# Opening of a two-layer backbone kernel: tokens loaded first, scale row before shift row, first block's products on unshifted tokens

## The chip, the cores and the metric

The kernel runs on 1 core of one Trainium2 chip. The metric is device time in microseconds (us) of that core. Three runs of the kernel before gave 941.29, 941.98 and 942.39, so the median is 941.98. TensorE (PE), VectorE (DVE), ScalarE (ACT), GpSimd (POOL) and SyncE (SP) each run their own instruction stream and wait for each other by semaphores.

## The reference, cut to what matters

Two layers over 256 latent and 256 context tokens of width 1024. The change concerns the start of layer 0 only:

```python
def modulate(h, shift, scale):
    return h * (1.0 + scale) + shift

mod_l = (c_act @ mod_w[i] + mod_b[i]).reshape(b, N_MOD, 1, d)      # latent tokens
mod_c = (c_ctx_act @ mod_w[i] + mod_b[i]).reshape(N_MOD, d)        # context tokens
hl = modulate(rms_norm(xl, norm_g[i, 0]), mod_l[:, 0], mod_l[:, 1])
hc = modulate(rms_norm(xc, norm_g[i, 0]), mod_c[0], mod_c[1])
u = h @ w_in                                                       # 1024 x 1536
y = a * jax.nn.sigmoid(g)            # a: columns 0..511 of u, g: columns 512..1023
# depthwise convolution of y, 31 taps, then layer_norm and silu;
# the last 512 columns of u go through a pooling mixer
# [y_conv | y_pool] @ w_out, gated residual, then a mixture of 32 experts; layer 1 follows
```

So each sub-layer needs a shift row (mod row 0) and a scale row (mod row 1), for latent and for context tokens, and each row is a product of the conditioning vector with a 1024 x 1024 matrix of 4 MB.

## The kernel before, in words

**Weights.** SP issues one stream of loads, in the order of `stream_plan`, nearly all of 2 MB. A unit `("mod", L, v, h)` is half of the matrix of mod row v of layer L; `("win", j)` is a third of the input matrix. The first seven units go into the seven slots of a ring at once; each later one waits until the products that read its slot are done (`slot_plan` picks the slot, the list `early` orders the first ones; `freed` names the semaphore). The four token tiles of 0.5 MB go down the same queue, behind the first unit.

**Opening.** PE turns the small parameter rows into columns (L1018 to L1020). ACT makes the sigmoid of the conditioning vectors (L1510), DVE turns it into their silu `cs` (L1882). ACT squares the tokens (L1522), POOL makes the reciprocal norms (L2266, L2267), DVE scales the tokens by them (L1931), PE turns them (`turn_pair`, L1096), and ACT and DVE copy the turned halves to `hT` (L1635, L2193). Between these PE makes the mod rows (`mod_part`, L1046, 8 products a unit), ACT copies a row (`mod_copy`, L1528), PE turns it (`mod_turn`, L1056), DVE adds the bias (`mod_columns`, L1890) and makes the scale `gsc` (L1924). Then ACT (even k, L1641) and DVE (odd k, L2201) apply scale and shift to `hT` in place, in eight instructions each.

**First block.** `value_gate(m, part)` makes 8 products of 128 x 128 x 512 for value (part 0) or gate (part 1) of channel block m (L1384; the profile counts two MATMUL records for each such product). ACT makes the sigmoid (L1649), DVE multiplies (L2208), and then runs the 31 taps of the convolution on DVE (L2217, L2219 and 29 times L2221) and adds the two accumulators (L2224). There are four blocks m, one after the other. PE meanwhile makes the products of the other blocks, the mod rows 2 to 5 and the pool part (L1397). POOL does the pooling (L2359 to L2365) while DVE is in its taps. When the last block is done, PE turns the result (L1448), DVE and POOL normalise, ACT applies silu (L1687, L1688), and PE makes the output product (L1437); routing and the experts follow.

Each engine works strictly in the order in which its part of the program is written out.

## Time and profile before

| what | value |
|---|---|
| median of 3 runs | 941.98 us (941.29 to 942.39) |
| profiled execution, its own time | 943.45 us |
| its span | 941.8 us |
| PE busy | 838.4 us (89%) |
| DVE busy | 364.3 us (39%) |
| ACT busy | 168.2 us (18%) |
| POOL busy | 178.0 us (19%) |
| chain of waits that ended last | PE 47%, DMA 24%, DVE 13% |
| read from memory | 293.67 MB, 325 GB/s over the span |

A row of a timeline gives start, length, engine, line, operation, what it writes and reads, how many, and in brackets the idle time of the engine before it with what ended it. "PEclk" is the granted TensorE clock as a share of 2.4 GHz, so 1.00 is 2.4 GHz and 0.50 is 1.2 GHz.

### The profile page before, as it was taken

To read this page: it belongs to the slowest core of one execution; us is meant where nothing else is said; L and a number is where in the kernel's file an instruction comes from. 1 tells how busy PE (TensorE), PEld (TensorE's weight loads), DVE (VectorE), ACT (ScalarE), POOL (GpSimd) and SP (SyncE) were. 2 spreads that over 40 slices of the span, in tenths; PEclk is the share of its full clock that TensorE was granted. 3 is DMA by queue.
4 is the path that set the end of the run, shared out by engine and by line. 5 is a ranking of instruction groups with operands and counts; after the bars stand their busy time and mean duration, and the time that the engine had idled before them with its cause. 6 is when DMAs were issued, how large, how long until landed. Compare 5 with 4: busy or idle time off the path is not lost.

```text
span 941.8 us, 10008 instructions
## 1 busy us (share of the span) xinstructions
PE 838.4 (89%) x3727; PEld 371.6 (39%) x3727; DVE 364.3 (39%) x764; ACT 168.2 (18%) x415; POOL 178.0 (19%) x214
## 2 busy tenths in 40 slices
PE   4899999999999999878849999889899999778785
PEld 2444445447433333222228444446445333222221
DVE  1269998217111221110223686648625111011010
ACT  2301012216100000000023111538323000000000
POOL 2100292131120222201131221400211111011001
PEclk9899999999999999999959999989999999889899
DMA  8999355617999999999989459310577999999994
GB/s 364 408 400 407 127 212 216 276 81 261 333 405 410 356 403 399 393 397 416 423 312 429 190 209 366 148 81 1 203 305 249 405 404 406 413 418 427 408 418 174
DMA packets 34038, 297.99 MB, mean 316 GB/s; under 512 B 6624, under 2 KB 6930, under 8 KB 16316
## 3 DMA queue, kind: packets, MB, share of 16 engines
q1 hardware_dynamic: 26928, 283.26, 74.7%
q0 software_dynamic: 6976, 13.93, 4.2%
q8 instruction: 38, 0.62, 0.3%
q14 instruction: 20, 0.16, 0.0%
q10 hardware_dynamic: 76, 0.02, 0.0%
HBM read 293.67 MB, written 12.58 MB: 325 GB/s over the span
## 4 chain that ended last, share of the span: by engine, by line
PE 47%; DMA 24%; DVE 13%; issue 5%; SPq 4%; ACT 3%; PEld 2%; POOL 1%; PEldq 0%; DVEq 0%; POOLq 0%; ACTq 0%
PE bank L1287 12%; DVE WORK L2221 10%; PE bank L496 9%; DMA ring<-in_gu_pack 8%; DMA ring<-in_down_pack 6%; PE bank L1312 5%; PE bank L1437 5%; DMA WORK<-in_gu_pack 4%; DMA ring<-in_win_pack 3%; PE bank L1162 3%; SPq L987 2%; PE bank L1384 2%; DMA h_rows<-B 1%; PE bank L553 1%; PE bank L562 1%
## 5 line engine op out<-in xcount | busy, mean ns | idle before, releaser
L1287 PE MATMUL bank<-ring,hT 128*64 128x512 f32 x704 | 217.4, 629 | 25.6 <-DMA ring<-in_gu_pack 12.9
L2135 DVE SCALAR_TENSOR_TENSOR hT<-hT,WORK,bank 128x256 f32<-128x256 f32 x34 | 16.3, 481 | 323.5 <-ACT hT L1587 310.8
L1287 PEld LDWEIGHTS bank<-ring,hT 128*64 128x64 f32 x704 | 63.9, 144 | 123.6 <-issue 122.9
L2221 DVE SCALAR_TENSOR_TENSOR WORK<-WORK,par 128x512 f32<-128x512 f32 x116 | 90.7, 861 | 0.0
L496 PE MATMUL bank<-ring,hT 128*128 128x512 f32 (+2 forms) x256 | 88.0, 499 | 0.7 <-ACT hT L1550 0.7
L1312 PE MATMUL bank<-ring,WORK 128*64 128x512 f32 x336 | 76.4, 596 | 4.3 <-DMA ring<-in_down_pack 3.3
L1287 PE MATMUL bank<-WORK,hT 128*64 128x512 f32 x128 | 63.7, 644 | 5.0 <-issue 3.5
L1592 ACT ACTIVATE WORK<-bank 128x256 f32<-128x256 f32 x34 | 13.0, 383 | 282.7 <-PE bank L1296 282.7
L1384 PE MATMUL bank<-hT,ring 128*128 128x512 f32 x128 | 58.9, 620 | 1.9 <-DMA ring<-in_win_pack 1.9
L496 PEld LDWEIGHTS bank<-ring,hT 128*128 128x128 f32 x256 | 46.0, 190 | 35.8 <-issue 34.0
L1437 PE MATMUL bank<-ring,B 128*128 128x512 f32 x128 | 56.6, 596 | 0.8 <-DVE B L2238 0.8
L869 POOL DMA_INDIRECT hT<-h_rows,smalli x21 | 20.1, 958 | 174.3 <-PE bank L1261 81.0
L1287 PE MATMUL bank<-X,hT 128*64 128x512 f32 x104 | 46.9, 595 | 5.2 <-DMA B<-in_gu_pack 2.8
L2266 POOL TENSOR_SCALAR small<-small 128x1 f32<-128x1 f32 (+2 forms) x46 | 13.5, 293 | 181.2 <-DVE small L1751 62.1
L1287 PE MATMUL bank<-B,hT 128*64 128x512 f32 x96 | 43.6, 597 | 1.0 <-issue 1.0
L1046 PE MATMUL bank<-ring,cs 128*32 128x512 f32 x256 | 33.9, 666 | 9.1 <-DMA ring<-in_mod_pack 7.8
L1312 PEld LDWEIGHTS bank<-ring,WORK 128*64 128x64 f32 x336 | 23.1, 137 | 47.0 <-issue 40.3
L1384 PEld LDWEIGHTS bank<-hT,ring 128*128 128x128 f32 x128 | 25.1, 199 | 34.2 <-issue 31.2
L882 POOL DMA_INDIRECT latents<-WORK,smalli x8 | 8.2, 1024 | 153.2 <-DVE WORK L2153 153.2
L2267 POOL TENSOR_TENSOR small<-small,cst 128x1 f32<-128x1 f32 (+2 forms) x46 | 35.7, 777 | 3.8
L1437 PEld LDWEIGHTS bank<-ring,B 128*128 128x128 f32 x128 | 23.8, 190 | 31.2 <-issue 27.7
L1587 ACT ACTIVATE hT<-bank 128x256 f32<-128x256 f32 x34 | 13.0, 383 | 125.0 <-PE bank L1287 121.1
(312 smaller groups left out, 1083.3 us busy)
## 6 DMA issues: line engine op xcount, KB each, us to landing
ring<-in_gu_pack SPq DMA_DIRECT2D x39, 2048.0 KB, 19.6
ring<-in_mod_pack SPq DMA_DIRECT2D x24, 2048.0 KB, 14.1
ring<-in_down_pack SPq DMA_DIRECT2D x19, 2048.0 KB, 31.9
WORK<-in_gu_pack SPq DMA_DIRECT2D x6, 2048.0 KB, 23.6
ring<-in_wout_pack SPq DMA_DIRECT2D x4, 2048.0 KB, 12.7
ring<-in_gu_pack SPq DMA_DIRECT2D x8, 1024.0 KB, 28.5
ring<-in_win_pack SPq DMA_DIRECT2D x3, 2048.0 KB, 37.2
X<-in_gu_pack SPq DMA_DIRECT2D x3, 2048.0 KB
```

What stands on the lines that cost most here:

```text
L496: mm = pe.matmul(dst[:, 0:hi - lo], hT[:, k, t * P:(t + 1) * P], w[:, k, :], start=k == 0, stop=k == KC - 1)
L869: return pool.indirect_dma_start(XG[s], None, h2d[:, :], bass.IndirectOffsetOnAxis(ap=smalli[0:ST, i:i + 1], axis=0), bounds_check=rows_ - ...
L987: sp.dma_start(dst, src).then_inc(sem(f"weights_in{at}"), 16)
L1046: mm = pe.matmul(bank[b][at:at + 32, :], cs[:, k, :], w, start=k < 2, stop=k >= KC - 2)
L1162: mm = pe.matmul(bank[OUT_BANKS[L][i % 2]][:, :], lhs(k, j), w[:, k, :], start=k == 0, stop=k == KC - 1)
L1287: mm = pe.matmul(dst[ST * x:ST * x + ST, :], HG[L][s][:, k, :], columns(units[x], 512 * k, 512), start=k == 0, stop=k == KC - 1)
L1312: mm = pe.matmul(bank[5 + s][ST * h:ST * h + ST, :], HET[s][:, f, ST * x:ST * x + ST], columns(n, 2048 * x + 1024 * f + 512 * h, 512), sta ...
L1384: mm = pe.matmul(b[:, :], w[:, k, 256 * part + P * (m % 2):256 * part + P * (m % 2) + P], hT[:, k, :], start=k == 0, stop=k == KC - 1)
L1437: mm = pe.matmul(bank[OUT_BANKS[0][i % 3]][:, :], mixT[:, (k + 4) % KC, j * P:(j + 1) * P], w[:, (k + 4) % KC, :], start=k == 0, stop=k == ...
L2135: dve.scalar_tensor_tensor(out=T1[L][s], in0=SG[L][s], scalar=cwt[:, at:at + 1], in1=src[:, 0:DE], op0=ALU.mult, op1=ALU.mult).then_inc(se ...
L2221: ins = dve.scalar_tensor_tensor(out=acc, in0=src, scalar=w, in1=acc, op0=ALU.mult, op1=ALU.add)
L2267: pool.tensor_tensor(dst, dst, C("half", 0, 1).to_broadcast([P, n]), ALU.pow).then_inc(sem(name), 1)
```

## The change

The stream of loads now begins with the tokens, then mod row 1 (scale), the first input unit, mod row 0 (shift), and the other two input units. `hT` gets only the scale at first. Block 0's products run on these unshifted tokens; the shift's own product with the weights of block 0 is made apart (`shift_products`: 8 products of 32 x 256; `shift_columns`: two of 128 x 2) and added per column in the sigmoid's bias and in the multiplication. The shift is then added to `hT` by ACT and DVE for the later blocks. Mod row 0 is multiplied in the middle of `value_gate(0, 0)`. On ACT the sigmoid of the conditioning now stands behind the four squares.

```diff
-    out = pair(0, 0) + pair(0, 1)
-    out += [("win", j) for j in range(3)]
+    out = pair(0, 1) + [("win", 0)] + pair(0, 0) + [("win", 1), ("win", 2)]
...
             for n, u in enumerate(STREAM):
-                if n == 1:
+                if n == 0:
                     for i in range(NT):
...
-            mod_multiply(0)
             turn_pair("a0", 0, range(KC))
+            pe.wait_ge(sem("par_ready"), 2)
+            mod_half(0, 0)
+            turn_pair("a0", 1, range(KC))
+            busy(5, 12)
+            mod_half(0, 1).then_inc(sem("mod_mm"), 1)
             mod_turn(0)
-            turn_pair("a0", 1, range(KC))
-            mod(1)
...
+            def shift_products():
+                pe.wait_ge(sem("mod_cols"), 2)
+                w = slot(where[("win", 0)])
+                for k in range(KC):
+                    at = 32 * (k % 4)
+                    mm = pe.matmul(bank[4][at:at + 32, 0:HALF], mods[:, 0, :, :, :].rearrange("p v k s -> p (v k s)")[:, 2 * k:2 * k + 32],
+                                   w[:, k, :].rearrange("p (a b c) -> p a b c", a=2, b=2)[:, :, 0], start=k < 4, stop=k >= 4)
+                mm.then_inc(sem("par_turned"), 1)
+            def shift_columns():
+                pe.wait_ge(sem("par_ready"), 3)
+                for part in range(2):
+                    mm = pe.matmul(bank[4][:, HALF + 2 * part:HALF + 2 * part + 2], shift_part[:, part * P:part * P + P], C("sel32", 0, 2), start=True, stop=True)
+                mm.then_inc(sem("par_turned"), 1)
...
-            for m in (0, 1):
-                value_gate(m, 1)
-                value_gate(m, 0)
+            value_gate(0, 1)
+            value_gate(0, 0, 4, lambda: mod_multiply(1))
+            mod_turn(1)
+            shift_products()
+            value_gate(1, 1, 3, shift_columns)
+            value_gate(1, 0)
...
-            act.wait_ge(sem("par_ready"), 1)
-            act.activation(csg[:, :], par[:, R_CCTX:R_CCTX + 16], ACT.Sigmoid).then_inc(sem("sig_done"), 1)
...
             square_rows("a0", range(4))
-            mod_copy(0)
+            act.wait_ge(sem("par_ready"), 1)
+            act.activation(csg[:, :], par[:, R_CCTX:R_CCTX + 16], ACT.Sigmoid).then_inc(sem("sig_done"), 1)
...
+            for k in range(0, KC, 2):
+                for s, lo, hi in stream_cols("a0"):
+                    act.activation(hT[:, k, lo:hi], hT[:, k, lo:hi], ACT.Identity, bias=mods[:, 0, 0, k, s:s + 1]).then_inc(sem("ht_0"), 1)
+                if k == 0:
+                    act.wait_ge(sem("par_turned"), 2)
+                    act.activation(shift_part, bank[4][:, 0:HALF], ACT.Copy).then_inc(sem("par_ready"), 1)
...
+                if m == 0:
+                    act.wait_ge(sem("par_ready"), 4)
+                    for s, lo, hi in stream_cols("a0"):
+                        ins = act.activation(SGL[0][:, lo:hi], bank[1][:, lo:hi], ACT.Sigmoid, bias=shift_in[:, 1, s:s + 1])
...
+            for k in range(1, KC, 2):
+                for s, lo, hi in stream_cols("a0"):
+                    ts(hT[:, k, lo:hi], hT[:, k, lo:hi], mods[:, 0, 0, k, s:s + 1], None, ALU.add).then_inc(sem("ht_1"), 1)
+                if k == 3:
+                    dve.wait_ge(sem("par_turned"), 3)
+                    dve.tensor_copy(mv[:, 0:4], bank[4][:, HALF:HALF + 4]).then_inc(sem("par_ready"), 1)
```

On PE, from the first products to the end of block 1 (L1046 mod rows, L1026 filling products, L1096 turning of tokens, L1056 turning of a mod row, L1384 block products), the program before has:

```order
4 L1046 MATMUL bank<-ring,cs 32x512 x8
5 L1026 MATMUL bank<-cst 128x128 x12
6 L1046 MATMUL bank<-ring,cs 32x512 x8
7 L1096 MATMUL bank<-cst,B 128x128 x16
8 L1056 MATMUL bank<-cst,MR 128x4 x4
9 L1096 MATMUL bank<-cst,B 128x128 x16
10 L1046 MATMUL bank<-ring,cs 32x512 x16
11 L1056 MATMUL bank<-cst,MR 128x4 x4
12 L1384 MATMUL bank<-hT,ring 128x512 x32
```

And the changed program has, at the same place on PE (L1048 mod rows, L1098 tokens, L1058 mod row turned, L1407 block products, L1382 and L1390 the shift's products):

```order
4 L1098 MATMUL bank<-cst,B 128x128 x16
5 L1048 MATMUL bank<-ring,cs 32x512 x8
6 L1098 MATMUL bank<-cst,B 128x128 x16
7 L1026 MATMUL bank<-cst 128x128 x12
8 L1048 MATMUL bank<-ring,cs 32x512 x8
9 L1058 MATMUL bank<-cst,MR 128x4 x4
10 L1407 MATMUL bank<-hT,ring 128x512 x12
11 L1048 MATMUL bank<-ring,cs 32x512 x16
12 L1407 MATMUL bank<-hT,ring 128x512 x4
13 L1058 MATMUL bank<-cst,MR 128x4 x4
14 L1382 MATMUL bank<-ring,mods 32x256 x8
15 L1407 MATMUL bank<-hT,ring 128x512 x3
```

The 16 products of the second mod row moved from ahead of the block products to behind the twelfth of them, and the first use of a mod unit moved behind the first 16 turnings of tokens.

On ACT, at the start, the program before has:

```order
11 L1510 ACT_TABLE_LOAD
12 L1510 ACTIVATE csg<-par 128x16
13 L1522 ACTIVATE B,small<-X 128x1024 x4
14 L1528 ACTIVATE MR<-bank 128x512
15 L1635 ACTIVATE hT<-bank 128x256 x8
```

The changed program has there:

```order
11 L1545 ACT_TABLE_LOAD
12 L1545 ACTIVATE B,small<-X 128x1024 x4
13 L1655 ACT_TABLE_LOAD
14 L1655 ACTIVATE csg<-par 128x16
15 L1659 ACTIVATE hT<-bank 128x256 x8
16 L1551 ACTIVATE MR<-bank 128x512
```

The sigmoid went behind the squares, and a second load of ACT's tables came with it.

On DVE, from the making of `cs` (L1922) to the first taps (L2276), the changed program has:

```order
9 L1922 TENSOR_TENSOR cs<-csg,par 128x2x8
10 L1971 TENSOR_SCALAR B<-X,small 128x1024 x4
11 L2233 COPY hT<-bank 128x256 x8
12 L1930 TENSOR_TENSOR mods<-bank,par 128x16
13 L1964 SCALAR_TENSOR_TENSOR gsc<-mods,par 128x8 x2
14 L2240 TENSOR_SCALAR hT<-hT,gsc 128x256 x8
15 L1930 TENSOR_TENSOR mods<-bank,par 128x16
16 L2247 TENSOR_SCALAR hT<-hT,mods 128x256 x4
17 L2250 COPY small<-bank 128x4
18 L2247 TENSOR_SCALAR hT<-hT,mods 128x256 x4
19 L2259 SCALAR_TENSOR_TENSOR WORK<-bank,small,WORK 128x256 x2
20 L2272 TENSOR_SCALAR WORK<-WORK,par 128x512
```

Rows 15 to 18 are new between the application of the scale and the first block's multiplication; the scaling of the tokens (row 10) still stands behind `cs` (row 9).

## Rows read from the trace of the kernel before

**Rows 1.** Busy tenths in 40 slices of the whole span.

```profile
PE   4899999999999999878849999889899999778785
...
DMA  8999355617999999999989459310577999999994
```

**Rows 2.** Chain that ended last, 30 to 60 us: start, length, what.

```profile
6.35 30.86 DMA ring<-in_win_pack
...
37.25 16.97 PE bank L1384 x32
...
54.31 0.70 DVE WORK L2208
...
55.04 0.55 DVE WORK L2217
```

**Rows 3.** The same chain, 118 to 175 us.

```profile
122.70 32.78 DVE WORK L2221 x29
...
156.26 1.97 PE bank L1448 x16
```

**Rows 4.** Timeline of PE, 140 to 175 us.

```profile
149.04 7.03 PE L1437 MATMUL bank<-ring,B 128*128 128x512 f32 x16
```

**Rows 5.** Busy time by stretch: us, PE, PEld, DVE, ACT, POOL, PEclk, DMA share, GB/s.

```profile
36.50:43.40 6.90, 6.15 (x8) 2.61 (x9) 2.09 (x7) 3.45 (x8) 0.00 (x0) 0.51 1.02 378
...
119.50:147.00 27.50, 26.78 (x123) 13.99 (x122) 27.43 (x21) 5.05 (x20) 25.18 (x17) 1.00 0.59 242
...
195.00:216.00 21.00, 21.00 (x72) 9.91 (x71) 3.70 (x6) 4.65 (x9) 6.58 (x9) 1.00 0.00 1
```

**Rows 6.** DMA issues at 2.1 to 2.3 us: count, KB each, us to landing.

```profile
ring<-in_mod_pack SPq DMA_DIRECT2D x1, 2048.0 KB, 8.9
```

**Rows 7.** Timeline, 0 to 25 us.

```profile
5.08 1.28 ACT L1510 ACT_TABLE_LOAD   x1 [5.08 <-issue]
...
14.37 3.64 PE L1046 MATMUL bank<-ring,cs 128*32 128x512 f32 x16 [1.23 <-DVE cs L1882]
...
16.34 1.06 ACT L1522 ACTIVATE B<-X 128x1024 f32<-128x1024 f32 x1 [2.32 <-DMA X<-in_x]
...
17.94 3.60 PE L1026 MATMUL bank<-cst 128*128 128x128 f32 x24
...
18.56 0.75 DVE L1931 TENSOR_SCALAR B<-X,small 128x1024 f32<-128x1024 f32 x1 [4.25 <-POOL small L2267]
...
20.42 0.19 ACT L1522 ACTIVATION_READ_ACCUMULATOR B<-X 128x1 f32 x1
```

**Rows 8.** Timeline, 23 to 72 us.

```profile
23.32 2.15 PE L1096 MATMUL bank<-cst,B 128*128 128x128 f32 x16
...
31.69 1.92 PE L1046 MATMUL bank<-ring,cs 128*32 128x512 f32 x16 [1.69 <-DMA ring<-in_mod_pack]
...
34.33 1.05 PE L1056 MATMUL bank<-cst,MR 128*128 128x4 f32 x8 [0.72 <-ACT MR L1528]
...
35.92 4.04 ACT L1641 ACTIVATE hT<-hT,mods,gsc 128x256 f32<-128x256 f32 x8 [1.64 <-DVE gsc L1924]
35.92 2.67 DVE L2201 TENSOR_SCALAR hT<-hT,gsc,mods 128x256 f32<-128x256 f32 x8
...
67.87 3.64 PE L1046 MATMUL bank<-ring,cs 128*32 128x512 f32 x32
```

**Rows 9.** Page, part 5, two groups: PSUM read by DVE and by ACT.

```profile
L2135 DVE SCALAR_TENSOR_TENSOR hT<-hT,WORK,bank 128x256 f32<-128x256 f32 x34 | 16.3, 481 | 323.5 <-ACT hT L1587 310.8
...
L1592 ACT ACTIVATE WORK<-bank 128x256 f32<-128x256 f32 x34 | 13.0, 383 | 282.7 <-PE bank L1296 282.7
```

**Rows 10.** Timeline of ACT, 695 to 698.5 us.

```profile
696.25 0.19 ACT L1522 ACTIVATION_READ_ACCUMULATOR WORK<-X 128x1 f32 x1
696.45 1.28 ACT L1707 ACT_TABLE_LOAD   x1
697.74 0.20 ACT L1707 ACTIVATE small<-small 128x1 f32<-128x1 f32 x1
```

More of the change, by code:

```diff
@@ L164, in slot_plan @@
     places, held, free = [], {}, list(range(RING))
-    early = [("mod", 0, 0, 0), ("mod", 0, 0, 1), ("mod", 0, 1, 0), ("mod", 0, 1, 1), ("win", 0), ("mod", 0, 2, 0), ("mod", 0, 2, 1),
+    early = [("mod", 0, 1, 0), ("mod", 0, 1, 1), ("mod", 0, 0, 0), ("mod", 0, 0, 1), ("win", 0), ("mod", 0, 2, 0), ("mod", 0, 2, 1),
              ("mod", 0, 3, 0), ("mod", 0, 3, 1), ("win", 1), ("mod", 0, 4, 0), ("mod", 0, 4, 1), ("win", 2), ("mod", 0, 5, 0), ("mod", 0, 5, 1),
@@ L392, in generator_kernel @@
         LNS = hT[:, 0:4, :]
+        shift_part = MR[:, 0, 0:HALF]
         stats = cut(24)
         mv = cut(8)
+        shift_in = mv[:, 0:4].rearrange("p (a s) -> p a s", a=2)
         lrs = cut(4)
@@ L924, in ht_before @@
         def ht_before(tag, i):
-            return {"a0": (0, 0), "m0": (16, 16), "a1": (28, 20), "m1": (36, 28)}[tag][i]
+            return {"a0": (0, 0), "m0": (24, 24), "a1": (36, 28), "m1": (44, 36)}[tag][i]
         RAW_BANKS = ((4, 6), (5, 7))
@@ L1026, in busy, with mod_half @@
                     pe.matmul(bank[b][:, 0:P], ident, ident, start=True, stop=True)
+            def mod_half(i, h):
+                loaded(pe, where[("mod",) + MOD_PAIRS[i] + (h,)])
+                return mod_part(i, MOD_BANK[i], range(4 * h, 4 * h + 4))
             def mod_multiply(i):
@@ L1033, in mod_multiply @@
                 for h in (0, 1):
-                    loaded(pe, where[("mod",) + MOD_PAIRS[i] + (h,)])
-                    mm = mod_part(i, MOD_BANK[i], range(4 * h, 4 * h + 4))
-                    if i == 0 and h == 0:
-                        busy(5, 12)
+                    mm = mod_half(i, h)
                 mm.then_inc(sem("mod_mm"), 1)
@@ L1381, in value_gate @@
                 for k in range(KC):
-                    if m == 0 and part == 1:
-                        pe.wait_ge(sem(f"ht_{k % 2}"), 10 + 2 * (k // 2))
+                    if m <= 1 and part == 1:
+                        pe.wait_ge(sem(f"ht_{k % 2}"), 8 * m + 10 + 2 * (k // 2))
+                    if k == at:
+                        middle()
                     mm = pe.matmul(b[:, :], w[:, k, 256 * part + P * (m % 2):256 * part + P * (m % 2) + P], hT[:, k, :],
@@ L1635, in _ @@
                 act.activation(hT[:, k, 256 * i:256 * i + 256], bank[u % 4][:, 0:HALF], ACT.Copy).then_inc(sem("ht_0"), 1)
-            mod_copy(1)
+            mod_copy(0)
             act.wait_ge(sem("gsc"), 1)
@@ L1640, in _ @@
                 for s, lo, hi in stream_cols("a0"):
-                    act.activation(hT[:, k, lo:hi], hT[:, k, lo:hi], ACT.Identity,
-                                   bias=mods[:, 0, 0, k, s:s + 1], scale=gsc[:, 0, 0, k, s:s + 1]).then_inc(sem("ht_0"), 1)
+                    act.activation(hT[:, k, lo:hi], hT[:, k, lo:hi], ACT.Identity, scale=gsc[:, 0, 0, k, s:s + 1]).then_inc(sem("ht_0"), 1)
+            mod_copy(1)
+            act.wait_ge(sem("mod_cols"), 2)
+            act.wait_ge(sem("ht_0"), 16)
+            act.wait_ge(sem("glu_mm"), 2)
+            for k in range(0, KC, 2):
[4 more added lines that the diff above has]
+                    act.activation(shift_part, bank[4][:, 0:HALF], ACT.Copy).then_inc(sem("par_ready"), 1)
             def glu_gate(m):
@@ L1871, in _ @@
             dve.memset(cs[:, :, :], 0.0)
+            dve.memset(mods[:, 0, 2, :, :], 0.0)
             dve.memset(YP[:, :, :, 0:PADC], 0.0)
@@ L2200, in _ @@
                 for s, lo, hi in stream_cols("a0"):
-                    ts(hT[:, k, lo:hi], hT[:, k, lo:hi], gsc[:, 0, 0, k, s:s + 1], mods[:, 0, 0, k, s:s + 1],
-                       ALU.mult, ALU.add).then_inc(sem("ht_1"), 1)
+                    ts(hT[:, k, lo:hi], hT[:, k, lo:hi], gsc[:, 0, 0, k, s:s + 1], None, ALU.mult).then_inc(sem("ht_1"), 1)
+            mod_columns(1)
+            dve.wait_ge(sem("mod_cols"), 2)
+            dve.wait_ge(sem("ht_1"), 16)
+            dve.wait_ge(sem("glu_mm"), 2)
+            for k in range(1, KC, 2):
[4 more added lines that the diff above has]
+                    dve.tensor_copy(mv[:, 0:4], bank[4][:, HALF:HALF + 4]).then_inc(sem("par_ready"), 1)
+            dve.wait_ge(sem("par_ready"), 4)
             for m in range(4):
@@ L2207, in _ @@
                 s3 = lambda x: x.rearrange("p (s t) -> p s t", s=2)
-                tt(YP[:, m, :, PADC:PADC + HALF], s3(bank[2 * (m % 2)][:, :]), s3(SGL[m % 2]), ALU.mult).then_inc(sem("glu_done"), 1)
+                if m == 0:
+                    for s, lo, hi in stream_cols("a0"):
+                        ins = dve.scalar_tensor_tensor(out=YP[:, 0, s, PADC:PADC + HALF], in0=bank[0][:, lo:hi], scalar=shift_in[:, 0, s:s + 1],
+                                                       in1=SGL[0][:, lo:hi], op0=ALU.add, op1=ALU.mult)
+                else:
+                    ins = tt(YP[:, m, :, PADC:PADC + HALF], s3(bank[2 * (m % 2)][:, :]), s3(SGL[m % 2]), ALU.mult)
+                ins.then_inc(sem("glu_done"), 1)
                 dve.wait_ge(sem("glu_done"), m + 1)
```

8 lines of the change are left out of this document (4 added, 4 removed).

## The prediction

> **What bounds the kernel now.** I read the page first: PE is at 90% or more in most slices, and the loads stop now and then in slices 5 to 9 [rows 1]. Then the chain of waits. At the start it is the stream of loads: the first input unit lands at 37.2, PE makes the 16 products of block 0 until 54.2, DVE starts the taps at 55.04 [rows 2]. From there to 156.2 it is DVE's taps alone, and then PE again, which turns their result at 156.26 [rows 3]. So a change of the opening is worth what it moves the first tap (55.04), provided that PE and POOL keep up. They do so barely: PE ends its own work ahead of the turning at 149.04 + 7.03 = 156.07 [rows 4], 0.2 us ahead of DVE. Hence an earlier first tap alone would gain next to nothing; a later one costs in full. The last block's 29 taps take 32.78 us [rows 3], because between 119.5 and 147 POOL works beside DVE; there DVE ends only some 21 instructions in 27.5 us [rows 5]. POOL starts when PE brings the first pool product, not when DVE is at some tap, so that loss stays as long as POOL's work falls into the taps, as it does here in both programs.
>
> What comes after 156 keeps its distance. From 195 to 216 no bytes move (0.00 share) while PE is busy all the time [rows 5]: the loads wait for slots, and the slots come free behind the work that hangs on the taps. The experts' loads, which bound much of the rest, start after that gap. I let the first tap's shift reach the end one for one.
>
> **The front, up to the scaled tokens.** Before, scaling starts at 35.92 [rows 8].
>
> - Tokens. The first 2 MB in the queue landed 8.9 us after an issue at 2.2, at 11.1 [rows 6]; the tokens, second, let ACT begin at 16.34 [rows 7]. First in the queue they should land at 11.4 (four issues for one: I add 0.3).
> - Squares: four from 16.34 to 20.61, 4.27 us [rows 7]. Now 11.4 to 15.7.
> - The sigmoid stands behind them, and ACT loads its tables a second time: 1.28 us [rows 7]. The first load was hidden in the wait for tokens, this one is not: nothing on ACT covers it. Sigmoid at 17.0, `cs` at 17.5. DVE's scaling of the tokens stands behind `cs` on DVE, so it starts at 17.55 instead of about 13.6 (11.4 + 18.56 - 16.34). Of the 5 us that the tokens gain, 4 are lost here. At 0.75 us each [rows 7] two tiles are scaled at 19.1.
> - PE, from 19.1, in order: 16 turnings 2.15, 8 products of the scale row 1.92, 16 turnings 2.15 [rows 8], 12 filling products, 8 products 1.92. The filling took 3.60 when PE was half of that time in its slow phase [rows 7]; at the pace of the turnings (0.12 each, 24 records) I take 2.8. That is 10.9. The slow phase adds to it: PE has been idle since 13.1, as it was ahead of 14.37, where 16 records took 3.64 against 1.92 later, to 18.0 [rows 7, 8]; the 24 filling records behind took 0.7 more than 24 x 0.12, so half pace went on for 1.4 more, to 19.4, 5 us in all. Five us at half pace cost 2.5. Less 0.4 for the overlaps of these rows: 32.1. The second scale half has landed long before (third in the queue, two spans of 5.2 behind 11.1, so 21.5; 5.2 is (37.2 - 11.1)/5 [rows 2, 6]).
> - From the end of a mod row's products to scaling: 35.92 - (31.69 + 1.92) = 2.3 [rows 8]. Scaling starts at 34.4, only 1.5 us earlier.
>
> **Block 0.** The first k is ready after two of ACT's eight (4.04/8 = 0.5 each [rows 8]): 35.4. The input unit is there at 26.7 (fourth: 11.1 + 3 x 5.2). A product takes 7.03/8 = 0.86 with its tail left off [rows 4]. Before, the granted clock was 0.51 from 36.5 to 43.4 [rows 5], the 1.2 GHz level, after a PE that had worked in snatches; that cost about 3.2 of the 16.97 us. I let it stay at 1.00 now. Twelve products: 45.7. Mod row 0's last half lands at 37.2 as before, since the same units are ahead; 8 us to spare. Its 16 products, which before ran ahead of block 0 in PE's wait for the unit, now stand in it: 3.6 [rows 8]. Four products: 52.7. So far 1.5 us better than 54.2.
>
> **The shift's tail,** all of it new between the products and the taps. Turning mod row 0 1.05 [rows 8]: 53.8. DVE's bias 0.25: 54.05. Now three engines hand to each other. PE's `shift_products` have no row: half the columns of the 1.92 case, so 0.5 to 1.9; I take 0.6. ACT adds the shift to k = 0 (1.0 us, to 55.05), and this hides them up to 1.0. Then ACT copies (0.38 [rows 9]) and adds k = 2: 56.45. PE has three products of block 1 to make ahead of `shift_columns`, the third waits for k = 2: 57.3; the two small ones 0.5: 57.8. DVE's copy 0.2: 58.0. Queued behind that copy on DVE are its last four additions (2.67/8 = 0.33 each [rows 8]): 59.4. ACT's last additions end at 58.5 and its two sigmoids at 59.3, beside them. Two multiplications of 128 x 256 with PSUM: between 0.33 and 0.48 each [rows 8, 9]; at 0.45, 60.3.
>
> So the first tap comes at 60.3 instead of 55.04: **5.3 us later**. The front gives 1.5 and the clock 3.2, the moved mod row takes 3.6, the tail 6.1 more than the 0.8 that stood there.
>
> **Later.** PE's stream changes less: block 1 follows at about 55 to 69 instead of 54.2 to 67.9, 1 us later, so POOL starts 1 us later and still ends well inside the taps (148 against 161). Block 1's products are there when DVE wants them at 81. Slots: the ring's first slots come free at 32 instead of 23.5, the next at 49 instead of 33.6; the seven first units fill the queue until about 50, and nine until past 57, so no gap arises.
>
> Sum: the profiled execution at 943.45 becomes 948.75. It was 1.5 above the median of 941.98, so for the median of runs I say 947.3.
>
> **A page weighed against a row.** In layer 1 the table load begins 0.01 us behind ACT's reading of an accumulator, and the next function 0.01 us behind the load: 1.3 from the one to the other [rows 10]. The Trainium skill (ScalarE: Activation LUTs, What ACT_TABLE_LOAD costs) puts a drain of about 1.38 us beside the load. By that page the forecast would be 1.4 us higher, an estimate; the trace shows no such drain.
>
> **Unknown costs.** Tokens landing: 9.5 (all bandwidth to them) to 12.5: -1.9 to +1.1. Slow phase: 3.5 to 7 us: -0.8 to +1. Shift products -0.1 to +0.9. Multiplications and sigmoids -0.3 to +0.4. Together about 945.0 to 949.5 without another clock.
>
> **Rivals.**
>
> *The clock drops again, 0.30.* Scaling is again preceded by idle stretches: 0.7 for the copy and 1.65 until the first k, with the turning between. Before, idle stretches of 1.7, 0.7 and 1.9 us [rows 8, 2] came ahead of the 0.51 [rows 5]. For: the same kind of snatches. Against: about half the idle time, and 12 filling products right ahead. A stretch as before costs 3.2: 950.5. The Trainium skill (TensorE: Matmul & The Clock Gate, HAM oscillation) describes such drops in kernels in which PE waits between bursts.
>
> *The front is really early, 0.09: faster.* If DVE's token scaling did not wait for the late sigmoid, PE would hang on the loads alone: second scale half at 21.5, + 1.92 + 2.3 = 25.7, which is 8.7 before my 34.4. From scaling to first tap I have 25.9 us, so the first tap would come at 51.6, and PE and POOL would come earlier too: 938.5. It decides from a scaling start before 29.1. Against it stands the order on DVE and ACT.
>
> *Nothing, 0.09.* The tail is shorter than I think (the additions overlap better, tokens land near 9.5, PE's slow phase is short): the terms' low ends sum to -2.5, and a start at 32 with a tail 2 us shorter gives 942 to 943.5. Also here: later stages swallow the shift. PE's reserve of 0.2 speaks against that.
>
> *The main case, 0.52:* 947.3, own range 944.5 to 949.5.
>
> **Numbers.** 0.2% (1.9 us) is about what a measurement of this kernel can tell from no change. Faster by more: 0.09. Within: 0.09, which goes to 943.9. Slower: 0.82. The range runs from 942.3, which takes in half of the case of nothing, to 951.3, past the drop of the clock.
>
> **What would show it.** First tap (L2272) near 60; table load behind the squares, DVE's token scaling not before 17; scaling (L2240) at 34 to 35; granted clock in 35 to 45; mod row 0's products between block 0's twelfth and thirteenth; DVE's copy L2250 near 58; turning of the result near 161.5 with PE waiting for it. Wrong it would be if scaling starts before 31, or if the first tap is late and the 195 to 216 gap in the loads is not shifted with it.

## The result and the profile after

The changed kernel took 952.6 us (median of four runs, 950.3 to 956.0), the kernel before 942.2 beside it on the same chip: a ratio of 1.0099, 95% interval 1.0076 to 1.0122. On two other chips the ratio was 1.0098 (1.0071 to 1.0125) and 1.0102 (1.0079 to 1.0125). The forecast was 947.3, with a range up to 951.3. The direction is right, the size is not: 9 to 10 us were lost where 5.3 were forecast.

The profiled execution of the changed kernel took 950.32 us, with a span of 948.7. Its page, busy tenths in 40 slices, as in [rows 1]:

```profile
PE   2999998999999999877949999879899999779785
...
PEclk9999999999999999989978999989999999889899
DMA  9999354626899999999979459420477999999994
```

PE is as full as before, and the loads pause in the same part of the span. The chain of waits (start us, us, what), which answers to [rows 2] and [rows 3]:

```profile
3.77 7.48 DMA X<-in_x
...
11.28 4.27 ACT B L1545 x8
...
15.56 1.28 ACT L1655
...
34.30 10.54 PE bank L1407 x24
44.84 3.57 PE bank L1048 x32
48.41 3.63 PE bank L1407 x8
...
59.42 0.55 DVE WORK L2272
...
127.09 32.80 DVE WORK L2276 x29
...
160.66 1.97 PE bank L1474 x16
```

The chain no longer starts with the input unit but with the tokens, their squares and the table load. The scale row, block 0 and the shift follow, and the first tap stands at 59.42 in place of 55.04. From there the taps take what they took: 160.66 - 59.42 = 101.24, before 156.26 - 55.04 = 101.22. The last block's 29 took 32.80 against 32.78. PE is no longer close behind them: it stands idle for 2.56 us before it can turn their result, and 0.19 us in the kernel before. The start of that row:

```profile
160.66 1.53 PE L1474 MATMUL bank<-cst,WORK 128*128 128x128 f32 x12 [2.56 <-DVE WORK L2279]
```

The timeline of the opening (start us, us, engine, line, operation, out<-in, count, idle time before):

```profile
15.56 1.28 ACT L1655 ACT_TABLE_LOAD   x1
...
17.27 2.73 DVE L1971 TENSOR_SCALAR B<-X,small 128x1024 f32<-128x1024 f32 x4
...
18.73 3.67 PE L1098 MATMUL bank<-cst,B 128*128 128x128 f32 x16 [7.57 <-DVE B L1971]
...
26.25 2.84 PE L1026 MATMUL bank<-cst 128*128 128x128 f32 x24
...
29.02 1.92 PE L1048 MATMUL bank<-ring,cs 128*32 128x512 f32 x16
...
33.24 3.30 ACT L1665 ACTIVATE hT<-hT,gsc 128x256 f32<-128x256 f32 x8 [1.64 <-DVE gsc L1964]
...
51.87 0.95 PE L1058 MATMUL bank<-cst,MR 128*128 128x4 f32 x8
...
53.07 0.91 ACT L1672 ACTIVATE hT<-hT,mods 128x256 f32<-128x256 f32 x2 [4.00 <-DVE mods L1930]
...
53.09 1.07 PE L1382 MATMUL bank<-ring,mods 128*32 128x256 f32 x16 [0.27 <-DVE mods L1930]
...
56.77 0.50 PE L1390 MATMUL bank<-cst,MR 128*128 128x2 f32 x4
...
57.31 0.16 DVE L2250 COPY small<-bank 128x4 f32<-128x4 f32 x1 [3.10 <-PE bank L1390]
57.39 1.13 DVE L2247 TENSOR_SCALAR hT<-hT,mods 128x256 f32<-128x256 f32 x4
...
58.51 0.88 DVE L2259 SCALAR_TENSOR_TENSOR WORK<-bank,small,WORK 128x256 f32<-128x256 f32 x2
```

This is the forecast's order of steps. And by stretch (us, then busy time of PE, PEld, DVE, ACT and POOL, granted clock, DMA share, GB/s), which answers to [rows 5]:

```profile
34.40:41.40 7.00, 7.00 (x17) 3.17 (x18) 1.04 (x4) 2.15 (x6) 0.00 (x0) 1.00 1.03 387
...
195.00:216.00 21.00, 21.00 (x50) 9.31 (x49) 3.39 (x5) 3.45 (x6) 6.35 (x8) 1.00 0.15 60
```

In this execution the granted clock stayed at 1.00 (2.4 GHz) where it was 0.51 before, and the pause of the loads has moved on: between 195 and 216 the loads' share is 0.15 where it was 0.00, and between 216 and 220 it is 0.00 where it was 0.72.

But 4.4 us at the first tap are 6.9 at the end (948.7 - 941.8). The other 2.5 come behind the turning of the result. The largest piece is the stretch from the experts' first products to the first store of layer 0's output. Of before:

```profile
237.66:275.20 37.54, 33.81 (x191) 13.30 (x192) 7.34 (x17) 3.71 (x8) 5.93 (x6) 1.00 0.97 357
275.20:941.80 666.60, 587.19 (x2596) 248.80 (x2592) 210.92 (x484) 109.73 (x281) 113.57 (x148) 0.95 0.82 329
```

Of the changed kernel:

```profile
242.10:281.40 39.30, 35.59 (x193) 13.89 (x194) 7.33 (x17) 3.71 (x8) 6.00 (x7) 0.96 0.94 340
281.40:948.70 667.30, 586.18 (x2596) 250.16 (x2592) 211.07 (x484) 109.80 (x281) 113.82 (x148) 0.95 0.82 328
```

The same work takes 1.8 us longer because the clock was low in it once, at 0.50 for 3.41 us from 254.84: 0.96 over the stretch against 1.00. Behind 281 both kernels need the same within 0.7.

### The profile page after: what moved, and what is told of

Its sections match the earlier page's. It is cut to its first block, busy times and chain, and to the rows that moved or that the text cites. A ratio compares the mean times of both kernels' runs of the same rounds, so it can differ in the third digit from the quotient of the medians.

```text
span 948.7 us, 10075 instructions
## 1 busy us (share of the span) xinstructions
PE 837.4 (88%) x3747; PEld 374.2 (39%) x3747; DVE 366.2 (39%) x775; ACT 172.7 (18%) x426; POOL 180.0 (19%) x214
## 4 chain that ended last, share of the span: by engine, by line
PE 49%; DMA 22%; DVE 13%; issue 5%; SPq 5%; ACT 4%; PEld 2%; POOL 1%; PEldq 0%; DVEq 0%; POOLq 0%; ACTq 0%
PE bank L1289 11%; DVE WORK L2276 10%; PE bank L497 9%; DMA ring<-in_gu_pack 8%; DMA ring<-in_down_pack 6%; PE bank L1314 5%; PE bank L1463 5%; DMA WORK<-in_gu_pack 4%; PE bank L1164 3%; SPq L988 3%; PE bank L1407 2%; PE bank L1098 1%; PE bank L1048 1%; DMA h_rows<-B 1%; PE bank L554 1%
## 5 line engine op out<-in xcount | busy, mean ns | idle before, releaser
L1289 PE MATMUL bank<-ring,hT 128*64 128x512 f32 x704 | 215.0, 630 | 27.2 <-DMA ring<-in_gu_pack 14.4
L2276 DVE SCALAR_TENSOR_TENSOR WORK<-WORK,par 128x512 f32<-128x512 f32 x116 | 90.8, 863 | 0.0
L497 PE MATMUL bank<-ring,hT 128*128 128x512 f32 (+2 forms) x256 | 89.9, 508 | 0.7 <-ACT hT L1573 0.7
L1289 PE MATMUL bank<-WORK,hT 128*64 128x512 f32 x128 | 60.3, 614 | 3.9 <-issue 2.4
L1407 PE MATMUL bank<-hT,ring 128*128 128x512 f32 x128 | 56.7, 597 | 1.6 <-ACT hT L1665 1.6
L2321 POOL TENSOR_SCALAR small<-small 128x1 f32<-128x1 f32 (+2 forms) x46 | 11.9, 258 | 177.7 <-DVE small L1790 64.5
L1048 PE MATMUL bank<-ring,cs 128*32 128x512 f32 x256 | 31.0, 620 | 6.2 <-DMA ring<-in_mod_pack 6.2
L1407 PEld LDWEIGHTS bank<-hT,ring 128*128 128x128 f32 x128 | 23.8, 190 | 31.8 <-issue 31.1
```

Source lines behind the costliest of these rows:

```text
L497: mm = pe.matmul(dst[:, 0:hi - lo], hT[:, k, t * P:(t + 1) * P], w[:, k, :], start=k == 0, stop=k == KC - 1)
L1048: mm = pe.matmul(bank[b][at:at + 32, :], cs[:, k, :], w, start=k < 2, stop=k >= KC - 2)
L1289: mm = pe.matmul(dst[ST * x:ST * x + ST, :], HG[L][s][:, k, :], columns(units[x], 512 * k, 512), start=k == 0, stop=k == KC - 1)
L1407: mm = pe.matmul(b[:, :], w[:, k, 256 * part + P * (m % 2):256 * part + P * (m % 2) + P], hT[:, k, :], start=k == 0, stop=k == KC - 1)
L2276: ins = dve.scalar_tensor_tensor(out=acc, in0=src, scalar=w, in1=acc, op0=ALU.mult, op1=ALU.add)
```

## The experiments

Three causes were to be told apart: the later first tap (moved mod row and the shift's tail), passed on one for one; something in the change that stretches what lies behind; and TensorE's clock, which falls in other places. Letters in the quoted expectations belong to the group of kernels that ran together. Medians are of the timed runs, and each ratio is against the kernel before on the same chip.

**The changed kernel again.** No edit.

> The changed kernel, unaltered, for a second profile and a firmer time. Its first profile had the first tap at 59.4 (4.4 us late), the turning of the result at 160.7 (4.4 us late), but the end 6.9 us late, and the four times lie 8 to 14 us above before. Theory A (the shift passes one for one, and the rest is TensorE's granted clock, which falls at other places in each execution): first tap at 59.4 +- 0.3 again, turning at 160.7, but the distance from there to the end differs from the first profile by 1 us or more. Theory B (the later stages stretch any shift of the opening in a fixed way): the same distance from the turning to the end as in the first profile, 788.0 us within 0.5. Theory C (in some executions the clock already drops in the opening, my rival): first tap near 62.6 in such a profile. Time 950 to 956.

952.64 (949.81 to 954.47), ratio 1.0098 (1.0071 to 1.0125). The profiled execution shows what the first one had not: the clock was 0.50 from 34.96 to 38.37, and the first tap came at 61.95, as theory C said. From the turning of the result to the end it took 787.8, within 0.5 of the first profile's 788.0; this is what theory B said, and only the later profiles tell the two apart.

**Tokens first and nothing else.** The kernel before, with the tokens queued ahead of the first input unit:

```diff
-                if n == 1:
+                if n == 0:
```

> The kernel before with the four token tiles ahead of the first weight unit and nothing else changed. Theory A (the first input unit at 37.2 bounds the products, whatever comes ahead): time as before within 1 us, products from 37.2; the granted clock ahead of them can differ, which is worth up to 3 us either way. Rival (tokens first helps by itself): 2 us or more below before.

941.85 (940.53 to 944.54), ratio 0.9991 (0.9974 to 1.0007). Scaling began at 35.70 against 35.92, since it hangs on mod rows that PE makes ahead; the low clock from 37.88 lasted 3.41 us instead of 6.83, and the first tap came at 53.44. So tokens in front alone make no difference that can be told: the interval goes from 2.5 us faster to 0.7 slower.

**The sigmoid ahead of the squares.** The changed kernel with one table load:

```diff
+            act.wait_ge(sem("par_ready"), 1)
+            act.activation(csg[:, :], par[:, R_CCTX:R_CCTX + 16], ACT.Sigmoid)...
             square_rows("a0", range(4))
-            (the same two lines)
```

> The changed kernel with the conditioning's sigmoid ahead of the squares again; one table load. Theory A (the late sigmoid with its table load holds DVE's token scaling back by 3 to 4 us, on the path): token scaling from 13.9 instead of 17.3, scale applied from 29.8 to 30.5 instead of 33.2, first tap at 56 to 56.7 instead of 59.4, time 2.5 to 4 us below the changed kernel. Rival (PE's slow phase or the loads take its place): scale applied no earlier than 32.5, time within 1 us of the changed kernel. The loads alone would allow 25.7.

951.64 (948.99 to 953.19), ratio 1.0088 (1.0062 to 1.0115): no gain that can be told. Its timeline:

```profile
13.86 0.75 DVE L1971 TENSOR_SCALAR B<-X,small 128x1024 f32<-128x1024 f32 x1 [1.82 <-POOL small L2322]
...
16.14 2.40 PE L1098 MATMUL bank<-cst,B 128*128 128x128 f32 x10 [5.28 <-DVE B L1971]
...
19.42 1.54 PE L1098 MATMUL bank<-cst,B 128*128 128x128 f32 x6 [0.88 <-DVE hT L2233]
...
20.89 3.47 PE L1048 MATMUL bank<-ring,cs 128*32 128x512 f32 x16
...
24.29 2.05 PE L1098 MATMUL bank<-cst,B 128*128 128x128 f32 x16
```

The tokens are scaled from 13.86 instead of 17.27, and nothing comes of it: PE begins at 16.14 and stays in its slow phase until 24 (16 records of L1048 take 3.47 here, 1.92 later). In between it waits for DVE, whose copies stand behind the scaling of all four tiles, and DVE waits for POOL's norms. The second turnings begin at 24.29 against 24.36, and scaling at 33.2 in both. So the forecast's "of the 5 us that the tokens gain, 4 are lost here" names the wrong loser: without the late sigmoid PE's slow phase takes them. One reservation: in this profile the clock fell for 3.41 us in block 0, and the first tap came at 61.05. The changed kernel's profile with such a fall (61.95, above) was 0.9 later, so a gain of about 1 us is not excluded; the medians differ by as much and cannot tell it.

**A plain delay.** The kernel before, with n chained memsets on DVE ahead of block 0's multiplication, 1.19 us from one to the next:

```diff
+                if m == 0:
+                    for _ in range(5):
+                        link(dve.memset(CV[:, 0:2, :], 0.0))
```

> The kernel before, with five chained DVE memsets of 128 x 1024 ahead of block 0's multiplication, so that only the first tap is later, by some 4 to 5 us; the opening, the stream of loads and PE's order are those of before. Theory A (one for one): time +4.5 over before, give or take 1.5 for the clock. Theory B (later stages stretch the shift): +8 to +10, as in the changed kernel. If the time stays within +-1 the later stages swallow a shift, and the changed kernel loses its time elsewhere.

> The kernel before with ten chained DVE memsets, which take 1.19 us each by delay5's profile, so 11.9 us, ahead of block 0's multiplication. One for one: time +11.9 +- 1.5 over before. Stretching by the later stages: +15 or more. Given back by PE's or the loads' slack: +9 or less. In delay5 5.95 us were put in and 6.1 (4.0 to 8.2) measured.

> The kernel before with five chained memsets of 128 x 1024 on VectorE ahead of block 0's scaling, 5.95 us by the earlier profile. Both theories: first tap near 59.9 in place of 54.5, so 948 to 950. Theory A: within 2 us of the changed kernel of this group. Theory B: 2 to 5 us under it.

> The kernel before with 5.95 us of memsets ahead of block 0's scaling, one more profile. Both theories: first tap 59.4 to 59.9. A: one low stretch between 250 and 290 us.

The timeline of DVE with five of them (the second run):

```profile
52.93 0.91 DVE L2209 MEMSET WORK<- 128x1024 f32 x1 [14.86 <-PE bank L1384]
54.13 0.91 DVE L2209 MEMSET WORK<- 128x1024 f32 x1 [0.28 <-DVE WORK L2209]
...
59.38 0.55 DVE L2220 TENSOR_SCALAR WORK<-WORK,par 128x512 f32<-128x512 f32 x1
```

Five memsets (5.95 us) gave 949.07 and, on another chip, 948.08: ratios 1.0065 (1.0043 to 1.0087) and 1.0058 (1.0041 to 1.0074), so +6.1 and +5.5 us. Ten (11.9 us) gave 955.96, ratio 1.0137 (1.0107 to 1.0167), +12.9. The third profile of five took 949.44. So the shift is passed on one for one within the intervals (4.1 to 8.2 and 3.9 to 7.0 us for 5.95, 10.1 to 15.7 for 11.9), as the forecast had it: neither are the 11.9 us swallowed, nor do 5.95 become the 9 to 10 of the changed kernel.

**The shift made early.** The changed kernel with the sigmoid ahead, mod row 0's products in front of the first value product, and all sixteen shift additions on ACT, behind block 0's sigmoids, so that nothing of block 0 waits for them; the second version also leaves the filling products out, which compute nothing:

```diff
-            value_gate(0, 0, 4, lambda: mod_multiply(1))
-            mod_turn(1)
-            shift_products()
-            value_gate(1, 1, 3, shift_columns)
+            value_gate(0, 0, {0: (lambda: mod_multiply(1),), 4: (lambda: mod_turn(1),),
+                              6: (shift_products,), 7: (shift_columns,)})
+            value_gate(1, 1)
...
-            busy(5, 12)
```

> The changed kernel with the sigmoid of the conditioning first and the shift's chain pulled into block 0's value products: mod row 0's products ahead of the first of them, its turning behind the fourth, shift_products behind the sixth, shift_columns behind the seventh; ACT then makes block 0's sigmoid while PE still works and makes all sixteen additions of the shift to hT, so DVE's first multiplication waits for PE alone. Theory A (the changed kernel is slower because 3.6 us of mod products plus a tail of about 6 us of hand-overs stand between the products' start and the taps): products from 34.3 or 35.3, 16 of them 13.7, 3.6 of mod row, 1.0 + 1.1 + 0.5 of turning and shift products, multiplication 0.9: first tap at 55.2 to 56.2 (plus 1.7 to 2.6 where the clock drops), which is 4 to 5 us ahead of the changed kernel; time 4 to 5.5 us below the changed kernel, 3 to 5 above before. Rival (ACT's sixteen additions now hold block 1's products and that comes back on PE and POOL): first tap as said, but the turning of the result not more than 2 us ahead of the changed kernel's.

> The same without the 12 filling products ahead of the scale row's second half. Theory A (PE's order is the chain of the front, so the filling's 2.8 us are on it): scale applied at 30.4 to 31.5, first tap 2.8 us ahead of early_shift, 52.4 to 53.5, time 1 to 3 us below early_shift and within 2 us of before. Rival (the filling pays for itself by the clock): a longer stretch at 0.5 of the granted clock in 30 to 45, first tap no more than 1 us ahead of early_shift.

Timelines, of the first version (up to 60 us, where nine of the sixteen additions had begun) and then of the second:

```profile
43.28 3.64 PE L1048 MATMUL bank<-ring,cs 128*32 128x512 f32 x32
...
56.64 3.70 ACT L1684 ACTIVATE hT<-hT,mods 128x256 f32<-128x256 f32 x9
...
57.70 0.55 DVE L2263 TENSOR_SCALAR WORK<-WORK,par 128x512 f32<-128x512 f32 x1
```

```profile
31.07 10.06 PE L1406 MATMUL bank<-hT,ring 128*128 128x512 f32 x16 [1.58 <-ACT hT L1662]
41.06 3.64 PE L1048 MATMUL bank<-ring,cs 128*32 128x512 f32 x32
...
55.48 0.55 DVE L2262 TENSOR_SCALAR WORK<-WORK,par 128x512 f32<-128x512 f32 x1
```

946.88 (943.79 to 949.56), ratio 1.0032 (1.0014 to 1.0050), first tap 57.70; and 943.76 (940.11 to 947.18), ratio 1.0004 (0.9985 to 1.0023), first tap 55.48. So more than half of the loss can be taken out by order alone: some 3.0 us over before are left (0.0032 x 943) of 9.2, with a first tap at 57.70. That profile was the slowest of the twelve executions (949.56), so its first tap is rather a late one. Without the filling, products begin 3.5 us earlier, the clock is low for 6.83 us (from 30.19) instead of 3.41, and the first tap still comes 2.2 earlier; 52.4 to 53.5 had been expected, and it came at 55.48. Whether the filling shortens the fall is not shown: there is one profile of each version, and the changed kernel, always with the filling, had falls of 0, 3.41 and 6.83 us. But even the best version only reaches the kernel before: mod row 0's 3.64 us stand in block 0's stream, where PE before did them ahead of it, while the input unit was still on its way.

**POOL kept out.** In the profiles POOL's first addition took 7.09 us before, 10.89 after, 13.0 with five memsets and 1.1 with ten, where the next one, from 121.43, took 11.20. The experiment lets one tap of the changed kernel (block 2, tap 20) wait for the tap right ahead of it; the others wait for the one before that, so that they run without a gap.

```diff
-                        dve.wait_ge(sem("sum_done"), m * TAPS + j - 1)
+                        dve.wait_ge(sem("sum_done"), m * TAPS + j - (0 if m == 2 and j == 20 else 1))
```

> The changed kernel, in which tap 20 of block 2 waits for the tap just ahead of it instead of the one before that, so DVE's pipeline empties once in the middle of a block. In the changed kernel POOL's first pooling addition took 10.9 us and ended 0.9 us into DVE's closing addition of block 2, in before 7.1 us with the same end; POOL's later additions take 1.1 to 1.6 us. Theory A (DVE's back-to-back taps keep POOL out until DVE's stream has a gap): the first addition ends within 1.5 us of tap 20, that is 4 to 7 us earlier, POOL ends as much earlier, and the later taps of block 2 stretch from 0.66 to 1.5 us. Theory B (the long first addition is a start-up cost of POOL): it ends at the block's end or takes the same 10.9 us as before. The time stays within 2 us of the changed kernel in both, since the number of POOL's additions beside DVE's taps stays the same.

POOL's timeline of the changed kernel:

```profile
112.94 10.89 POOL L2414 TENSOR_TENSOR GB<-WORK 128x542 f32<-128x542 f32 x1 [81.72 <-ACT WORK L1693]
```

and DVE's:

```profile
103.58 19.30 DVE L2276 SCALAR_TENSOR_TENSOR WORK<-WORK,par 128x512 f32<-128x512 f32 x29
122.91 1.46 DVE L2279 TENSOR_TENSOR WORK<-WORK 128x512 f32<-128x512 f32 x1
```

POOL's timeline with the gap:

```profile
112.85 3.58 POOL L2414 TENSOR_TENSOR GB<-WORK 128x542 f32<-128x542 f32 x1 [81.73 <-ACT WORK L1693]
...
123.35 1.09 POOL L2414 TENSOR_TENSOR GB<-WORK 128x542 f32<-128x542 f32 x1 [3.74 <-ACT WORK L1693]
```

and the chain of waits there:

```profile
109.53 5.97 DVE WORK L2276 x9
115.50 0.02 issue
115.53 12.46 DVE WORK L2276 x11
```

The addition ended at 116.43, 0.93 us behind the gap at 115.50; in the changed kernel at 123.83, 0.94 behind the gap of 0.02 us at 122.89, where the block's taps end. The made pause let POOL in 7.4 us earlier. But a pause is not the only way in: the row at 123.35 took 1.09 in the middle of taps without any gap, and so did the first addition with ten memsets (1.12 from 110.93). What lets POOL in there is not shown. Once in, it slows the taps: 11 taps took 12.46, 1.13 each, against 0.66 (19.23/29). POOL's last addition ended 2.8 us earlier (147.27 against 150.05), and this brought nothing: 953.66 (949.98 to 958.46), ratio 1.0130 (1.0100 to 1.0161). The Trainium skill (SBUF — State Buffer, Who interferes with whom) says that a VectorE instruction with two inputs in SBUF contends with a GpSimd instruction that reads SBUF, over a shared port pair that is an exclusive lock. The trace agrees that one can keep the other out, and shows more than one instruction of waiting: at 0.66 each, some 15 taps passed before POOL's turn came in the changed kernel.

**What stays behind the shift.** More profiles of the three kernels (changed, before, and five memsets), no new edits, the fifth timed beside the delay kernel.

> The changed kernel, a third profile. So far: first tap at 59.42 without and at 61.95 with a low clock in the opening; from the turning of the result to the end 788.0 and 787.7. In four profiles of programs with the opening of before (with or without a delay) that distance was 783.3, 785.3, 785.4 and 785.5, and 788.6 in a fifth. Theory A (the distance depends on where the clock falls in that execution, the program has no part in it): over the further profiles of the changed kernel it spreads over 783 to 789 as in the others. Theory B (something in the changed program stretches the later stages by some 2 us): 787 or more again.

> The changed kernel, a fourth profile, as in changed_third: theory A expects a distance from the turning of the result to the end that differs from 787.9 by more than 1 us in at least one of the two, theory B 787 to 789 in both. Theory C (the opening's clock falls in most executions): first tap near 62 rather than 59.4.

> The changed kernel as it stands. Theory A (a shift of the first tap, passed on, and the clock of later stages as any shift brings it): the same time as the delay kernel of this group within 2 us, about 950. Theory B (something the change does behind the first tap, in the block with the added shift): 2 to 5 us above the delay kernel, with the distance from the first turning of the taps' sums to the end of the span 2 us or more above that kernel's.

> The changed kernel, one more profile. Theory A (the excess over the shift is the clock of later stages): two low stretches between 250 and 290 us and 39.3 us from the first product behind the attention to the first store of layer 0's output, where one stretch leaves 37.5 to 39.4. Theory C (chance of few profiles): one low stretch here as in before, and the first tap anywhere from 59 to 63.

> The changed kernel, one more profile. Both theories as for the sixth: A says two low stretches between 250 and 290 us again, C says one in about half the cases.

> The kernel before, unaltered, for a second profile. In its first one the clock was at 0.5 for 6.8 us from 36.5 and the first tap at 55.04; delay5 and tokens_first_only had 3.4 us there and would have had 53.9 and 53.4. Theory A (the opening's clock differs from execution to execution, and my base of 55.04 was a late one): a low stretch of 3.4 us and a first tap near 53.9 here. Otherwise 55.0 again, and then the first profile was typical.

> The kernel before, a third profile. So far first taps at 55.04 and 54.62, both with 6.8 us at half clock in the opening, and distances from the turning to the end of 785.5 and 788.6. Theory A: any distance from 783 to 789; theory B: 786 or less. First tap 53.4 to 55.1.

> The kernel before, one more profile. Both theories: first tap 53.9 to 55.0. A: one low stretch between 250 and 290 us.

What they show, each profile by itself (the distance is from the turning of the taps' sums to the end of the span):

| kernel | time, profiled | first tap | distance | start of a low clock at or just ahead of layer 0's first experts |
|---|---|---|---|---|
| changed, first | 950.3 | 59.42 | 788.0 | 254.8 |
| again | 952.6 | 61.95 | 787.8 | 256.8 |
| third | 951.5 | 59.12 | 789.5 | 254.0 |
| fourth | 947.6 | 59.08 | 785.6 | 253.9 |
| fifth | 953.4 | 63.24 | 787.3 | 259.6 |
| sixth | 948.2 | 59.48 | 785.9 | 254.9 |
| seventh | 950.5 | 59.55 | 788.1 | 234.3 |
| before, first | 943.5 | 55.04 | 785.6 | none |
| again | 946.2 | 54.62 | 788.6 | 250.6 |
| third | 942.2 | 53.92 | 785.3 | none |
| fourth | 944.5 | 53.26 | 788.4 | 248.8 |
| delay5 | 946.0 | 59.85 | 783.3 | 255.9 |
| delay5 again | 948.1 | 59.38 | 785.8 | none |
| delay5 third | 949.4 | 59.64 | 786.9 | none |

The fifth took 952.84 (949.48 to 955.82), the delay kernel beside it 948.08. That is 4.8 us, where theory A had at most 2; theory B had the 2 to 5, but also a distance 2 us or more longer, and it was 1.5 (787.3 against 785.8). The profiled executions of the two are 5.3 apart, of which the first taps (63.24 and 59.38) make 3.9. Neither theory holds as it was put.

Two readings. First, the opening has two courses. In five of seven profiles of the changed kernel the clock stays at 1.00 and the first tap comes at 59.1 to 59.6; in two it falls as block 0's products begin. (The kernel with the gap in the taps, whose opening is the same, stayed at 1.00 too, first tap 59.34.) By stretch, of the fifth:

```profile
34.46:41.29 6.83, 6.17 (x8) 2.62 (x9) 1.80 (x7) 2.91 (x8) 0.00 (x0) 0.51 0.99 375
```

and PE's timeline:

```profile
35.12 13.53 PE L1407 MATMUL bank<-hT,ring 128*128 128x512 f32 x24 [1.58 <-ACT hT L1665]
```

The 24 records took 13.53 there and 10.54 in the first profile, and the first tap came at 63.24. The two courses part before block 0: the first 8 products of the scale row, right behind the first turnings, took 3.08 and 2.61 in the two, and 1.92 to 2.10 in the five. PE of the second profile:

```profile
22.33 3.08 PE L1048 MATMUL bank<-ring,cs 128*32 128x512 f32 x16
```

So block 0's products begin about 1 us later there (35.28 and 35.12, against 34.20 in the mean of the five), and the low clock of 3.41 and 6.83 us costs the other 1.5 and 3.0. In before the clock falls in all four, for 6.83 us in two and 3.41 in two. The Trainium skill (TensorE: Matmul & The Clock Gate, What's actually happening) says that the point at which the clock first rises varies from run to run, with where in the chip's own rhythm the first product lands. The traces agree in that one kernel shows both an early and a late rise; no run here shows that rhythm, or why the late rise went with a fall in both cases.

Second, the distance has its own scatter of 3 to 4 us in each kernel. One step of it is plain: wherever the clock falls between the experts' first products and the first store, that stretch takes 39.2 to 39.4 us, and 37.5 to 37.6 where it does not, in all three kernels. The delay kernel without such a fall:

```profile
242.00:279.60 37.60, 33.84 (x193) 13.34 (x194) 7.35 (x17) 3.71 (x8) 5.94 (x6) 1.00 0.95 349
```

The changed kernel had it there in six profiles, and just ahead in the seventh (which costs 1.6 in the stretch before); before in two of four, the delay kernel in one of three. The larger part of the scatter lies behind that store: from there to the end it took 665.0 to 668.8 in the changed kernel, 666.4 to 667.8 in before and 662.7 to 667.9 in the delay kernel, and nothing here traces it to a cause.

The expectation of two low stretches in the changed kernel between 250 and 290 failed: the sixth had one, the seventh none. And a larger distance behind the taps is not shown: the means are 787.5 (seven), 787.0 (four) and 785.3 (three), within the scatter; but so few profiles do not exclude a microsecond or two.

## Why the prediction was wrong

The steps up to the first tap, forecast against the first profile after:

| step | forecast | measured |
|---|---|---|
| squares begin, end | 11.4, 15.7 | 11.28, 15.54 |
| DVE scales tokens | 17.55 | 17.27 |
| PE begins, last scale product ends | 19.1, 32.1 | 18.73, 30.94 |
| scaling begins, block 0's products | 34.4, 35.4 | 33.24, 34.30 |
| block 0's products end | 52.7 | 52.0 |
| mod row 0 turned | 53.8 | 52.8 |
| shift columns done | 57.8 | 57.3 |
| last additions end | 59.4 | 58.5 |
| first tap | 60.3 | 59.42 |

**Right.** The order of the steps, and most of their sizes. Table load without a drain: 15.56 + 1.28, sigmoid at 16.86. The mod row's 3.6 in block 0's stream: 3.57. The tail: 59.42 - 52.0 = 7.4, forecast 7.6. POOL a microsecond later: 0.6. One for one: the delays show it within their intervals. The mean of the seven first taps is 60.26, which is luck in part: the five without a fall were 1 us earlier than forecast, the two with one 2.3 later in the mean.

**Mis-sized: PE's slow phase.** I had it at 5 us; in the first profile it lasted 4.0, from 18.73 to 22.7, little longer than the first 16 turnings (3.67). That, with a start of PE 0.4 earlier, made the front 1.2 us earlier. The reason that I gave for the 4 lost microseconds was wrong too, as the early sigmoid showed.

**Half right: "I let it stay at 1.00 now",** as the likeliest case. It holds for five of seven profiles, but the course with a fall costs 2.6 to 3.9 at the first tap against the other five's mean of 59.33, about 1 of it in the front. The rival had this, at 0.30 and 3.2 us: 950.5, still under the measured time.

**Wrong: "What comes after 156 keeps its distance",** taken from one profile at 785.6. That was at the low end of before's own four (785.3 to 788.6), and the changed kernel's mean is 787.5. This is 1.9 of the error, and 1.6 to 1.8 of it is the one fall at 234 to 260, which all seven had.

**Wrong: 1.5 taken off for the median.** The profiled execution before had been 1.5 above its median, so I took the same off the changed one. The seven profiled executions of the changed kernel are at 950.6 in the mean, the 13 timed ones without a profile at 952.8: they are 2.2 above, not 1.5 below. The sign of one execution's distance to its median says nothing of another kernel.

So 947.3 becomes 952.6 by 1.5 for the median, 1.9 for the distance, and 1.9 by which timed executions exceed profiled ones. The first tap adds nothing to this by its mean, since the shorter front made up for the falls of the clock. The steps that failed are the distance of 785.6 and the 1.5 less for the median, and for two of seven profiles the clock at 1.00.

**The base was one profile too.** The forecast took its 5.3 from a first tap at 55.04; before's four have a mean of 54.2, so the shift in the means is 6.1. By profiled executions alone the change costs 6.5 (950.6 against 944.1), by timed ones 9 to 10.

**Slips in the sums.** The closing line's terms (front 1.5, clock 3.2, mod row 3.6, tail 6.1) give 5.0 and not 5.3. From the steps, block 0's products begin 1.85 earlier (37.25 - 35.4) and take 0.4 longer, and the tail is 7.6 in place of 0.84, 6.8 more. The low ends of the unknown costs sum to -3.1, not -2.5.

**What stays open** is that last piece. Executions without a profile leave no timeline, only their mean granted clock. It says something: it is 0.9624 in the mean of the seven profiled ones and 0.9585 in the other 13, and over all twenty an execution with 0.01 less clock was 4.4 us longer (a fitted line, correlation -0.71). So the profiled ones had more clock than usual; by that line this is worth 1.7 of the 2.2, an estimate. Where in the kernel it is lost the mean does not tell. If most of them took the slower course of the opening, the shift would be 62.6 - 54.2 = 8.4, and with 0.9 for the fall in the experts' start (1.8 in half the cases more) 9.3, as measured; and both profiled executions with that course (952.55 and 953.42) do lie at the timed ones' mean. This fits, and is not shown. Nor is shown why the delay kernel, with the same first tap as the changed one's five (59.6 and 59.3), is 4.8 us faster when timed beside it, and 3.6 on the other chip. Its clock falls in the opening in all three profiles, so no slower course of it was seen; and its mean distance, 785.3 from three profiles, is 2.2 shorter than the changed kernel's. No profile shows a step behind the taps that the change alone lengthens, and none excludes a small one.

## What to carry to other kernels

A step moved out of another engine's or a load's wait into the stream that feeds the critical engine costs its full time there (3.6 us here), and corrections added behind the products cost a tail of hand-overs between engines (7.4 us here): read the wait that covers a step before moving it. Where PE works in snatches, price both courses of its clock, in the opening and in each later stage that a shift reaches, from several profiles rather than one. And do not carry the distance between one profiled execution and its median over to another kernel.

## What was not expected of the hardware

- POOL's elementwise addition was held up for 2.5 to 12 us by VectorE's taps without a gap between them, and ended 0.93 us behind the first pause of 0.02 us: 7.09, 10.89, 13.0 and 3.58 us for the same instruction, of which about 1 is its own time. In other places it got in at once (1.12 and 1.09 us) with no pause between the taps.
- One program has two courses in its opening: after the same 3.67 us of first turnings, the next 16 records of L1048 took 2.10 us in the first profile and 3.08 in the second, and only in the second did the clock fall to 0.50 near block 0's start (34.96). With the turnings in two pieces from 16.14, the same records took 3.47.
- One fall of the clock to 0.50 for 3.41 us made a stretch of 37.6 us 1.7 longer, and where it fell differed from execution to execution of the same kernel.
- ACT's addition of a column to 128 x 256 in SBUF took 0.41 us (3.70/9), DVE's 0.28 (1.13/4).
